# Output products by block, tokens fetched as rows and turned, norms handed over in halves

## What is computed

```python
h = layer_norm_2(h, emb_g, emb_b)
for m in range(2):
    proj = h @ w_in[m] + ...             # q, k, v of two attentions, two gates
    merged = gate_a * (o_na @ w_na) + gate_b * (o_sw @ w_sw)
    h = layer_norm_2(ALPHA * h + merged @ w_out[m], ln1_g[m], ln1_b[m])
    f = swiglu_dense(h) if m == 0 else moe(h)      # 8 experts, top 2
    h = layer_norm_2(ALPHA * h + f, ln2_g[m], ln2_b[m])
```

## Time and profile before

| what | value |
|---|---|
| median of 3 runs | 2141.72 us (2138.93 to 2142.01) |
| the profiled execution's own time | 2138.8 us |
| span of its trace | 2137.0 us |
| PE busy | 98% of the span |
| DVE, ACT busy | 72%, 55% |
| granted TensorE clock, mean over the span | 0.993 |
| HBM traffic over the span | 252 GB/s |

### The profile page before, as it was taken

The page is one execution under the profiler, slowest core; times in us unless marked ns, Lnnn a source line. Parts: engine busy times, 40 slices in busy tenths (PEclk is TensorE's granted clock), DMA queues, the critical chain, the costliest instruction groups (busy, mean ns, idle before and its releaser), DMA issues.

```text
span 2137.0 us, 33255 instructions
## 1 busy us (share of the span) xinstructions
PE 2097.1 (98%) x12608; PEld 1837.3 (86%) x12608; DVE 1544.6 (72%) x1829; ACT 1177.6 (55%) x1204; POOL 13.3 (1%) x24
## 2 busy tenths in 40 slices
PE   9999999999999899999999999999999999999997
PEld 8888899999898899989887888888888888888885
DVE  8776356555555644454658989898998989899897
ACT  4302245434346333434717777776777777777774
POOL 0000000000000000000000000000000000000000
PEclk9999999999999999999999999999999999999999
DMA  8343443545552455555246989898998989899893
GB/s 327 140 143 133 172 156 127 193 180 188 228 176 97 158 180 178 191 223 178 100 157 264 379 346 362 342 365 347 364 369 344 363 335 370 346 366 360 349 359 154
DMA packets 76182, 540.03 MB, mean 253 GB/s; under 512 B 9136, under 2 KB 9280, under 8 KB 11952
## 3 DMA queue, kind: packets, MB, share of 16 engines
q1 hardware_dynamic: 71856, 522.22, 63.5%
q0 software_dynamic: 2080, 10.40, 1.3%
q10 hardware_dynamic: 2144, 5.93, 0.7%
HBM read 537.47 MB, written 1.05 MB: 252 GB/s over the span
## 4 chain that ended last, share of the span: by engine, by line
PE 88%; DVE 8%; issue 2%; ACT 2%; DVEq 1%; ACTq 0%
PE psum L1353 14%; PE psum L939 12%; PE psum L1330 10%; PE psum L1333 10%; PE psum L1334 10%; PE psum L779 6%; PE psum L952 5%; PE psum L751 5%; PE psum L715 4%; PE psum L702 2%; DVE scan_t L2268 2%; DVE big L2274 1%; DVE scan_t L2271 1%; PE psum L764 1%; PE psum L1285 1%
## 5 line engine op out<-in xcount | busy, mean ns | idle before, releaser
L2495 DVE TENSOR_TENSOR w_l<-ring,w_h 128x2048 fp32r<-128x2048 f32 x336 | 768.7, 2290 | 104.5 <-ACT w_h L1534 98.7
L1534 ACT ACTIVATE w_h<-ring 128x2048 fp32r<-128x2048 f32 x336 | 646.1, 1923 | 131.8 <-PE psum L1330 92.5
L1330 PE MATMUL psum<-w_h,xe_h 128*128 128x512 f32 x896 | 359.4, 401 | 0.9 <-DVE w_l L2495 0.9
L1334 PE MATMUL psum<-w_h,xe_l 128*128 128x512 f32 x896 | 349.8, 390 | 0.0
L1333 PE MATMUL psum<-w_l,xe_h 128*128 128x512 f32 x896 | 349.8, 390 | 0.0
L2087 DVE TENSOR_TENSOR wf_l<-ring,wf_h 128x2048 fp32r<-128x2048 f32 x66 | 151.1, 2291 | 135.6 <-ACT wf_h L1525 135.6
L2058 DVE TENSOR_TENSOR wp_l<-ring,wp_h 128x2048 fp32r<-128x2048 f32 x52 | 119.0, 2290 | 116.3 <-ACT wp_h L1548 116.3
L1330 PEld LDWEIGHTS psum<-w_h,xe_h 128*128 128x128 f32 x896 | 168.2, 188 | 37.1 <-DVE w_l L2495 3.9
L1334 PEld LDWEIGHTS psum<-w_h,xe_l 128*128 128x128 f32 x896 | 168.2, 188 | 36.2
L939 PE MATMUL psum<-xf_h,wf_h 128*128 128x256 f32 x688 | 195.7, 285 | 1.7 <-DVE xf_l L2095 1.7
L1333 PEld LDWEIGHTS psum<-w_l,xe_h 128*128 128x128 f32 x896 | 168.7, 188 | 31.9
(11 more groups left out here) (442 smaller groups left out, 3635.0 us busy)
## 6 DMA issues: line engine op xcount, KB each, us to landing
ring<-in_stream SPq DMA_DIRECT2D x497, 1024.0 KB, 6.1
big<-in_bc POOLq DMA_DIRECT2D x11, 512.0 KB, 7.3
big<-in_na_bias POOLq DMA_DIRECT2D x2, 2048.0 KB, 9.0
h<-in_x SPq DMA_DIRECT2D x2, 512.0 KB, 4.2
big<-in_mem ACTq DMA_DIRECT2D x1, 1024.0 KB, 12.8
big<-in_s_c ACTq DMA_DIRECT2D x1, 1024.0 KB, 17.3
r_k<-in_sgu_ln ACTq DMA_DIRECT2D x1, 1024.0 KB, 21.8
out_dram<-ysum ACTq DMA_DIRECT2D x2, 512.0 KB, 2.7
```

Source lines behind the costliest of these rows:

```text
L1330: first = nc.tensor.matmul(out, xe_h[:, k, :], wh[:, i, :], start=(k == 0), stop=False)
L1334: last = nc.tensor.matmul(out, xe_l[:, k, :], wh[:, i, :], start=False, stop=(k == KD - 1))
L1534: nc.scalar.activation(high, src, ACT.Copy).then_inc(w_high, 1)
L2495: V.tensor_tensor(low, src, high.bitcast(F32), ALU.subtract).then_inc(w_split, 1)
```

## The change

1. **Norms in halves.** The last step of a block norm is two operations of 128x512. The first raises the new semaphore `xn_half`, the second `xn_ready`. `normed_transposes` takes the place of `block_transposes` at the four joins: it turns the first half block after `xn_half`, the second after `xn_ready`.
2. **Second block turned within the products of the first** (`t_in0`, `t_in1`). The transposes of block 1 are issued in the middle of the product of block 0 with `w_in` chunk 1, between its contraction steps 3 and 4.
3. **Output groups 2 and 3 by block.** `out2` is gone; `last0` and `last1` each hold 512 columns (chunks `w_out` 2 and 3 of one block). The split of `w_out` 3 gets another buffer (`LENT`: slot 2 of `wf_h` and `wf_l`) and waits for no unit.
4. **Tokens fetched as rows.** In the seven gathers inside the loop, `pick` is the loaded operand and 512 columns of `h_h` or `h_l` stream past it (`pick_rows`: 8 products of 128x512 in place of 32 of 128x128). ACT copies the rows out of PSUM (`move_rows`, placed before the split of chunk down 12), and after up 13 PE turns them with 8 transposes (`turn_rows`). The first gather stays as it was.

```diff
-        out += [(("k8", f"w_out_{m}", i), (f"out{m}", i) if i < 3 else (f"last{m}", TB - 1)) for i in range(4)]
+        out += [(("k8", f"w_out_{m}", i), (f"out{m}", i) if i < 2 else (f"last{m}", TB - 1)) for i in range(4)]
...
-        add(f"out{m}", 3)
+        add(f"out{m}", 2)
...
+LENT = [SPLIT_AT[("k8", f"w_out_{m}", 3)] for m in range(2)]
...
+        picked_rows = big[:, 8192:9216]
...
+        xn_half = sem("xn_half")
...
+        rows_picked = sem("rows_picked")
+        rows_moved = sem("rows_moved")
...
+            if n in LENT:
+                return wf_h[:, 2, :], wf_l[:, 2, :]
...
                     for k in range(4):
                         last = nc.tensor.transpose(bank(u)[:, k * P:(k + 1) * P],
                                                    src[:, b, (4 * half + k) * P:(4 * half + k + 1) * P], ident[:, :])
+                    close_unit(last, u)
+            def normed_transposes(u0, b, n):
+                for half in range(2):
+                    pe.wait_ge(xn_ready if half else xn_half, n + 1)
+                    u = (u0, 2 * b + half)
+                    open_unit(pe, u)
+                    for k in range(4):
+                        last = nc.tensor.transpose(bank(u)[:, k * P:(k + 1) * P],
+                                                   h[:, b, (4 * half + k) * P:(4 * half + k + 1) * P], ident[:, :])
                     close_unit(last, u)
             def form_a(unit, chunk, act_T):
...
-            def split_b_block(unit, chunk, b, at, x_h=xf_h, x_l=xf_l, turned=None, filled=None):
+            def split_b_block(unit, chunk, b, at, x_h=xf_h, x_l=xf_l, turned=None, filled=None, halfway=None):
...
+                    if halfway is not None and k == KD // 2:
+                        halfway()
...
-                for b in range(TB):
-                    pe.wait_ge(acc_free, 2 * m + b + 1)
-                    pe.wait_ge(xn_ready, 1 + 4 * m + b)
-                    block_transposes(f"t_in{m}", h, b)
-                    for i in range(2):
-                        if b == 0:
-                            open_unit(pe, (f"projb{m}", i))
-                        last = split_b_block((f"projb{m}", i), ("k8", f"w_in_{m}", i), b, b,
-                                             turned=f"t_in{m}" if i == 0 else None)
-                        if b == TB - 1:
-                            close_unit(last, (f"projb{m}", i))
+                def second_block():
+                    pe.wait_ge(acc_free, 2 * m + 2)
+                    normed_transposes(f"t_in{m}", 1, 4 * m + 1)
+                pe.wait_ge(acc_free, 2 * m + 1)
+                normed_transposes(f"t_in{m}", 0, 4 * m)
+                for b, i in ((0, 0), (0, 1), (1, 0), (1, 1)):
+                    if b == 0:
+                        open_unit(pe, (f"projb{m}", i))
+                    last = split_b_block((f"projb{m}", i), ("k8", f"w_in_{m}", i), b, b,
+                                         turned=f"t_in{m}" if i == 0 else None,
+                                         halfway=second_block if (b, i) == (0, 1) else None)
+                    if b == TB - 1:
+                        close_unit(last, (f"projb{m}", i))
...
-                for i in range(1, 3):
-                    split_b((f"out{m}", i), ("k8", f"w_out_{m}", i))
+                split_b((f"out{m}", 1), ("k8", f"w_out_{m}", 1))
...
-                    close_unit(split_b_block((f"last{m}", b), ("k8", f"w_out_{m}", 3), b, 0), (f"last{m}", b))
+                    for i in range(2):
+                        last = split_b_block((f"last{m}", b), ("k8", f"w_out_{m}", 2 + i), b, i)
+                    close_unit(last, (f"last{m}", b))
...
-                        pe.wait_ge(xn_ready, 3 + b)
-                        block_transposes("t_mid0", h, b)
+                        normed_transposes("t_mid0", b, 2 + b)
...
-                pe.wait_ge(xn_ready, 7 + b)
-                block_transposes("t_mid1", h, b)
+                normed_transposes("t_mid1", b, 6 + b)
...
-            def gather(n):
+            def first_gather():
                 for k in range(KD):
                     for b in range(TB):
...
-                            if n == 0 and k == b == 0 and part is h_h:
+                            if k == b == 0 and part is h_h:
...
-                    if n == 0 and k == 3:
+                    if k == 3:
...
+                last.then_inc(gathered, 1)
+            def pick_rows():
+                for b in range(TB):
+                    for part in (h_h, h_l):
+                        for c in range(2):
+                            last = nc.tensor.matmul(psum[:, 6 + c, :], pick[:, b, :], part[:, b, c * 512:(c + 1) * 512],
+                                                    start=(b == 0 and part is h_h), stop=(b == 1 and part is h_l),
+                                                    skip_group_check=True)
+                last.then_inc(rows_picked, 1)
+            def turn_rows(n):
+                pe.wait_ge(rows_moved, n)
+                for k in range(KD):
+                    last = nc.tensor.transpose(psum[:, 6 + k // 4, (k % 4) * P:(k % 4 + 1) * P],
+                                               picked_rows[:, k * P:(k + 1) * P], ident[:, :])
...
                         pe.wait_ge(pick_ready, p + 2)
                         pe.wait_ge(y_added, p * 4 + 4)
-                        gather(1)
+                        pick_rows()
                     if s == LAST:
+                        if not last_pass:
+                            turn_rows(p + 1)
                         transpose_h(p, s - 1)
                     if s >= 2:
                         if s == 2 and not first:
...
-            gather(0)
+            first_gather()
...
-                elif n >= 2:
+                elif n >= 2 and n not in LENT:
...
+            def move_rows(n):
+                act.wait_ge(rows_picked, n)
+                nc.scalar.activation(picked_rows.rearrange("p (c d) -> p c d", c=2), psum[:, 6:8, :],
+                                     ACT.Copy).then_inc(rows_moved, 1)
...
+                    if (part, s) == ("gate", LAST) and not last_pass:
+                        move_rows(p + 1)
...
-                V.scalar_tensor_tensor(x[:, b, :], x[:, b, :], rstd[:, b:b + 1], b_, ALU.mult, ALU.add
-                                       ).then_inc(xn_ready, 1)
+                for half, ready in enumerate((xn_half, xn_ready)):
+                    cols = slice(512 * half, 512 * half + 512)
+                    V.scalar_tensor_tensor(x[:, b, cols], x[:, b, cols], rstd[:, b:b + 1], b_[:, cols],
+                                           ALU.mult, ALU.add).then_inc(ready, 1)
...
-                V.scalar_tensor_tensor(h[:, b, :], h[:, b, :], rstd[:, one], bc[:, 3, :], ALU.mult, ALU.add
-                                       ).then_inc(xn_ready, 1)
+                for half, ready in enumerate((xn_half, xn_ready)):
+                    cols = slice(512 * half, 512 * half + 512)
+                    V.scalar_tensor_tensor(h[:, b, cols], h[:, b, cols], rstd[:, one], bc[:, 3, cols],
+                                           ALU.mult, ALU.add).then_inc(ready, 1)
...
-                for i in range(3):
-                    if i < 2:
-                        wp_rest()
+                for i in range(2):
+                    wp_rest()
...
-                evacuated(dve, (f"out{m}", 2))
...
-                    hs = h[:, b, 768:1024]
-                    free_unit(V.scalar_tensor_tensor(hs, hs, ALPHA, bank(u)[:, 0:256], ALU.mult, ALU.add), u)
+                    hs = h[:, b, 512:1024]
+                    free_unit(V.scalar_tensor_tensor(hs, hs, ALPHA, bank(u), ALU.mult, ALU.add), u)
```

## The result

The median after is 2124.64 us (4 runs, 2123.30 to 2125.39), against 2141.8 for the four runs of before that go with it (2138.93 to 2142.01). The ratio is 0.992, with a 95% interval of 0.991 to 0.994: faster, by 17.2 us where 10.7 were forecast. The range began at 2126.0. The kernel before has executions of two kinds (experiment 1), and three of its four runs here are of the dearer one; against the cheaper kind alone, 2138.1, the gain is 13.5.

The account below looks back on a forecast made before the run. PE sets the pace in the experts' loop; at the joins it stands still for DVE and ACT. Terms 5.8 + 1.2 + 1.4 + 1.9 + 0.4 = 10.7 us off the median 2141.7 gave 2131.0, range 2126 to 2138.

Parts of the forecast that it names:

- Fetch as rows: Seven expert handovers: PE pays 2.69 us (products 1.81, transposes 0.88) in place of 3.52; 0.83 less each, 5.8 in all.
- First block and clock at t_mid1: At t_mid1 only PE's wait of 0.42 us before block 1's transposes can go: 0.4 us saved.
- The shift by 2.9 to the median: Whole kernel: the median shown, 2141.7 us, is 2.9 above the profiled execution; forecast set against it, 2131.0 rather than 2128.1.
- The row product's price: Each 512-column product of `pick_rows` at the handovers: 0.226 us by the nearest trace row, taken; other bound 0.44.
- The copy: At each handover ACT's added copy out of PSUM, 1.02 us, is covered by 2.0 us of PE's work; counted as nothing.
- The rival of the copy: At the handovers ACT does not absorb its copy: each costs 0.19 us more, total 2138.1, no difference; chance 0.1.
- the slower one: PE stands at `turn_rows` for ACT, 2.1 us per handover needed; total 2146 or more; chance 0.04.
- t_in0, 1.2: At t_in0, turning block 1 within block 0's products removes 1.3 us, less 0.1 and 0.07: 1.2 saved.
- t_mid0, 1.9: At t_mid0 the norm's second half comes 1.35 us earlier, four transposes ahead of it give 0.5: together 1.9.
- The rival of the clock: Low-clock stretches added at t_mid0 and t_in1 take back 4 us: 2135, chance 0.1; t_mid0's stretch going instead gives 2129.

Follow-up runs that it names:

- experiment 1: The kernel before, unchanged and measured again: 2141.96 us (12 runs), ratio 1.001.
- Experiment 9: The kernel before with one more group of dummy products at t_mid1, filling PE's wait of 0.42 us: 2136.97 us (11 runs), ratio 0.999.
- experiment 3: The kernel after with the gather of before put back (parts 1 to 3 of the change alone): 2131.31 us, ratio 0.996.
- experiment 4: The kernel after, with `turn_rows` turning only the first of the eight pieces at each handover: 2118.88 us, ratio 0.990.
- experiment 5: The kernel before with part 3 of the change alone (output groups 2 and 3 by block): 2134.67 us (11 runs), ratio 0.998.
- experiment 6: The kernel before with parts 1 and 2 alone (norms in halves, second block turned within the first's products): 2133.63 us, ratio 0.997.
- experiment 7: The kernel after with a second, unread copy by ACT of the fetched rows out of PSUM: 2124.00 us, ratio 0.993.
- experiment 8: The kernel after with dummy products of 512 columns in PE's idle times, three at t_in0 and five at t_mid0: 2120.93 us, ratio 0.991.
- experiment 2: The kernel before with part 4 of the change alone (tokens fetched as rows, copied, turned): 2131.71 us, ratio 0.996.

## Why the prediction was right or wrong

**The direction and the mechanisms held.** Fetch as rows, the second block within the products, output groups by block and the norm in halves each gave what its paragraph says or more, and no cost came back. What failed is the size, and in three terms. Of the 14.0 us between the profiles the terms gave 10.7; the 3.3 that they lack are 2.0 at t_mid1, 1.2 at the handovers and 0.8 of luck at the start, less 0.6 that t_in0 and t_mid0 gave too little.

**First block and clock at t_mid1, "That is all that can go: 0.4"; measured 2.4.** This is the step that failed most. I counted the wait of 0.42 and not what stood behind it. The earlier trace rows has eight transposes in 1.85 us, which take 1.04 at full clock, and the dummy product behind them takes 1.91 for 1.02. That is 0.8 + 0.9, with the wait 2.1; 0.3 more lies in the rest of the join. The dummy product before and after:

```profile
1121.34 1.91 PE L1243 MATMUL psum<-big,ident 128*128 128x512 f32 x2
```

```profile
1115.37 1.02 PE L1266 MATMUL psum<-big,ident 128*128 128x512 f32 x2
```

I asked for the lower clock at t_in0 and t_mid0 only, where the idle time was 2 to 3 us. Experiment 9 shows that the wait of 0.42 brings it here: filled, with nothing else changed, the transposes take 1.07.

**The shift by 2.9 to the median.** I took the 2.9 us between the profiled execution and the median of three runs as a constant. It was the gap between two kinds of execution of the kernel before, 4.0 by their medians. The kernel after has only one kind (2123.3 to 2125.4), as have experiments 3 to 9, which all lack the wait of 0.42, so far as 4 to 11 runs each tell. So its profiled span of 2123.0, 1.8 around it, is its median of 2124.6, and the dear kind's share of the gap is gained too. Experiments 1 and 9 show the place of most of it, t_mid1 again. How large that share comes out is luck of the draw: three of the four runs beside the result are of the dear kind, nine of the twelve of experiment 1, but 17 of the 48 others. The forecast without the 2.9 would have been 2128.1, and 2124.64 is below the range in either case. This is 3 of the 6.4 us by which the forecast was off (the sum of the terms is the other 3.3); the three runs (2138.93 beside 2141.72 and 2142.01) had shown the two kinds.

**Fetch as rows, "0.83 less per handover"; measured 1.00.** The two priced parts are right: pick 3.52 to 1.82, transposes 0.87. What was left out is the work right behind. The twelve products with chunk down 10 take 2.84 us behind the old gather and 2.72 behind the new one. Products and weight loads at that point, before:

```profile
1981.46 0.27 PE L1285 MATMUL psum<-pick,h_h 128*128 128x128 f32 x1
1981.51 0.19 PEld L1285 LDWEIGHTS psum<-pick,h_l 128*128 128x128 f32 x1
1981.57 0.28 PE L1285 MATMUL psum<-pick,h_l 128*128 128x128 f32 x1
1981.62 0.30 PEld L1353 LDWEIGHTS psum<-w_h,eT_h 128*128 128x128 f32 x2
1981.98 0.42 PEld L1353 LDWEIGHTS psum<-w_l,eT_h 128*128 128x128 f32 x2
```

and after:

```profile
1966.33 0.41 PEld L1322 LDWEIGHTS psum<-h_l,pick 128*128 128x128 f32 x2
1966.79 0.41 PEld L1393 LDWEIGHTS psum<-w_h,eT_h 128*128 128x128 f32 x2
1967.24 0.41 PEld L1393 LDWEIGHTS psum<-w_l,eT_h 128*128 128x128 f32 x2
```

After, a weight load of 0.19 starts 0.22 ahead of its product, under 512 columns. Before, it starts 0.06 ahead, and the pairs of products that follow are 0.53, 0.47, 0.45, 0.47, 0.46 and 0.46 apart, where after they are 0.45 or 0.46. With 0.05 less from the transposes to the next gate 0 this makes 0.99 in the trace of the last handover. That the late weight loads are the cause is read from these rows, and not tried; it stays open. Experiments 2 and 4 show that the 1.00 belongs to part 4 alone, and that the transposes' part of it is 0.108 each.

**The row product's price.** Of the bounds 0.226 and 0.44 the first is right, 1.82 us for eight. By the sustained figure of the Trainium skill (TensorE: Matmul & The Clock Gate, section Back-to-back issue gap), 131 ns, eight are an estimated 1.05; by its isolated 216 ns, 1.73. The traces of before and after have no two products of 512 columns less than 0.224 apart, and the isolated figure is 5% below the measured 0.227.

**The copy.** Right: covered by 2.2 us, and by more than another copy (experiment 7). The rival of the copy falls with it, and so does the slower one, which asked that PE stand at `turn_rows`.

**t_in0, 1.2; measured 0.7.** The idle 1.16 us went as written: from block 1's first transpose to the next product it is 0.79 us for 2.20, 1.4 less, and the first product of block 0 starts 0.13 later. The low clock lies over 23 products here and over 16 in the profile of before, and that gives back 0.6. How many it covers changes from one execution to the next: with the new code at this join five traces (after, experiments 3, 4, 6, 7) have 15.55 to 16.73, mean 16.2, and with the old code five (before, 1, 2, 5, 9) 16.71 to 18.00, mean 17.2. By the means the term is 1.0; one pair of profiles can't tell it closer than half a microsecond.

**t_mid0, 1.9; measured 1.8.** The first dense product comes 2.3 nearer, 0.4 more than forecast, since the transposes of block 1 are now over before the clock falls (granted 1.00 from 736 to 738, 0.67 from 738 to 739; they take 1.32, with a short wait between the halves, for 1.97). Five dense products more lie in the low stretch behind, and that takes it back. By means as above (17.3 of four, 19.2 of four) it is 1.9 to 2.0. Experiments 5 and 6 have 1.4 of it for the groups by block and 0.4 for the halves, for the 1.35 and 0.5 of the prediction.

**The rival of the clock** named the right mechanism. No stretch of low clock was added; one went, at t_mid1, where it was not looked for, and the one at t_mid0 stayed.

## What to carry to other kernels

Read the duration of one form in every place where it stands, and not only the idle marks: the same transposes at 1.04 and 1.85 us say that the clock has fallen, and if a short wait brought that, as here, the wait's price is several times the wait. Where a median and the profiled execution differ by more than the runs of one kernel scatter, ask first whether there are two kinds of execution, and which of them the profile is; a change that removes the cause also gains the difference. And where an operand can be either the loaded or the streamed one, stream the wide one: four products of 128 columns cost twice one of 512 here, enough to pay for the transposes that the swap asks for.

## What had not been expected of the hardware

A wait of PE of 0.42 us decides at t_mid1 over the lower clock: it follows in the three traces that have this wait (before, experiments 1 and 2) and in none of the eight others. The length of the wait alone does not tell it. At t_in1 the kernel before waits 0.41 and then 1.17 us, and the granted clock is 1.00 from 925 to 945; after 1124 it waits 0.65 us ahead of the first gather, and the clock stays. At t_mid1 sixteen products of 8 columns stand right ahead of the wait, but no run tried whether that matters. Once low, the clock stayed so for 3.4 us in one execution of a kernel and for 10.2 in another, by the shares of the microseconds shown in experiment 1, with PE busy for 10.00 of 10.00 us in the longer one.

Eight dummy products of 0.86 us each, in time that PE had to spend idle, took 3.9 us off the span and 3.1 to 3.7 off the median (experiment 8). And a run of 128-column products 0.110 apart, with weight loads of 0.19, is followed by 0.12 us more in the twelve products behind it.
